# Block 2's gated product over its accumulator in PSUM, rounded and split from there

## The reference

```python
h = rms_norm(x, norm_ffn_g[i])
a, b = jnp.split(h @ w_ffn_in[i], 2, axis=-1)
x = x + ((jax.nn.silu(a) * b) @ w_ffn_out[i]).astype(x.dtype)
```

## Time and profile before

| | |
|---|---|
| median of the runs | 2480.93 us |
| lowest, highest | 2478.26, 2481.35 us |
| profiled execution | 2478.87 us, span 2477.1 us |
| PE busy | 2179.5 us, 88% of the span |
| DVE busy | 739.9 us, 30% |
| ACT, POOL busy | 1089.7, 1606.8 us |
| mean granted clock of TensorE | 0.944 |

### The profile page before, as it was taken

How to read it: one execution, slowest core, us unless ns; L and a number is a source line. 1 busy time by engine, 2 the same in 40 slices (tenths; PEclk the granted TensorE clock), 3 DMA queues, 4 the chain that set the end, 5 groups by cost and what they waited for, 6 DMA issues and landing times.

```text
span 2477.1 us, 39464 instructions
## 1 busy us (share of the span) xinstructions
PE 2179.5 (88%) x13078; PEld 1925.1 (78%) x13078; DVE 739.9 (30%) x1595; ACT 1089.7 (44%) x2051; POOL 1606.8 (65%) x1281
## 2 busy tenths in 40 slices
PE   6698799997779799959998988899899998987997
PEld 6588699786768599749777877799697687776996
DVE  2221344036440344033221153221141310542221
ACT  3344465454134355434442364444344423653543
POOL 5285688881267488849784414699697853236996
PEclk9899899997989999979999899899899998998999
DMA  6533355531024255455435311455354345223553
GB/s 218 119 136 136 100 173 171 199 137 68 1 92 153 97 165 176 153 179 184 149 144 168 128 69 69 136 172 187 138 180 161 136 158 170 69 69 102 175 189 123
DMA packets 217288, 343.66 MB, mean 139 GB/s; under 512 B 8417, under 2 KB 124217, under 8 KB 216955
## 3 DMA queue, kind: packets, MB, share of 16 engines
q1 hardware_dynamic: 206059, 331.59, 39.0%
q10 hardware_dynamic: 11024, 9.45, 1.8%
HBM read 336.83 MB, written 4.19 MB: 138 GB/s over the span
## 4 chain that ended last, share of the span: by engine, by line
PE 75%; issue 6%; DVE 5%; DMA 4%; PEld 3%; ACT 2%; POOL 1%; DVEq 1%; PEldq 1%; ACTq 1%; SPq 0%; POOLq 0%
PE bank L669 11%; PE bank L672 11%; PE bank L673 11%; PE bank L687 7%; PE bank L691 7%; PE bank L690 7%; PE bank L711 3%; PE bank L714 3%; PE bank L715 3%; DMA ring<-in_w_in 2%; DMA distance_table<-PT 1%; PE bank L762 1%; PE bank L833 1%; POOL w_lo L1311 1%; PE bank L792 1%
## 5 line engine op out<-in xcount | busy, mean ns | idle before, releaser
L1311 POOL TENSOR_TENSOR w_lo<-ring,w_hi 128x512 fp32r<-128x512 f32 x1184 | 1548.3, 1321 | 660.3 <-ACT w_hi L1400 596.1
L1400 ACT ACTIVATE w_hi<-ring 128x512 fp32r<-128x512 f32 x1184 | 740.0, 631 | 958.2 <-PE bank L669 395.8
L669 PE MATMUL bank<-x_hi,w_hi 128*128 128x256 f32 x2080 | 602.6, 290 | 49.7 <-DVE x_lo L1829 21.1
L672 PE MATMUL bank<-x_lo,w_hi 128*128 128x256 f32 x2080 | 599.9, 288 | 0.0
L673 PE MATMUL bank<-x_hi,w_lo 128*128 128x256 f32 x2080 | 599.6, 288 | 0.0
L669 PEld LDWEIGHTS bank<-x_hi,w_hi 128*128 128x128 f32 x2080 | 411.6, 198 | 54.1 <-issue 31.1
L672 PEld LDWEIGHTS bank<-x_lo,w_hi 128*128 128x128 f32 x2080 | 411.9, 198 | 0.0
L673 PEld LDWEIGHTS bank<-x_hi,w_lo 128*128 128x128 f32 x2080 | 411.1, 198 | 0.0
L687 PE MATMUL bank<-w_hi,x_hi 128*128 128x512 f32 x720 | 293.2, 407 | 33.5 <-POOL w_lo L1311 13.7
L690 PE MATMUL bank<-w_lo,x_hi 128*128 128x512 f32 x720 | 287.1, 399 | 0.0
L691 PE MATMUL bank<-w_hi,x_lo 128*128 128x512 f32 x720 | 286.7, 398 | 0.0
(11 more groups left out here) (287 smaller groups left out, 2355.5 us busy)
## 6 DMA issues: line engine op xcount, KB each, us to landing
ring<-in_w_in SPq DMA_DIRECT2D x72, 1024.0 KB, 7.1
ring<-in_ffn_w_up SPq DMA_DIRECT2D x44, 1024.0 KB, 7.5
ring<-in_w_ffn_in SPq DMA_DIRECT2D x44, 1024.0 KB, 7.4
ring<-in_ffn_w_down SPq DMA_DIRECT2D x20, 1024.0 KB, 6.0
ring<-in_w_ffn_out SPq DMA_DIRECT2D x20, 1024.0 KB, 6.2
ring<-in_xattn_wkv SPq DMA_DIRECT2D x16, 1024.0 KB, 6.3
ring<-in_w_o_ret SPq DMA_DIRECT2D x16, 1024.0 KB, 6.0
ring<-in_od_w_in SPq DMA_DIRECT2D x12, 1024.0 KB, 6.3
```

What stands on the lines that cost most here:

```text
L669: m = mm(out_, view(w_hi)[:, k, :], x_hi[:, 4 * kh + k, :], start=p % 2 == 0 and k == 0, stop=False)
L672: mm(out_, view(w_hi)[:, k, :], x_lo[:, 4 * kh + k, :], start=False, stop=False)
L1311: tt(view(w_lo), src, view(w_hi), ALU.subtract).then_inc(w_lo_ready, 1)
L1400: return A(o, i_, ACT.Copy, **kw)
```

## The change

In block 2 the product is written over the linear half in its own bank. The rounding and the remainder read it there. The bank is given free by the remainder, not by the product, and `ff_h` by a one-element copy behind a third drain. Block 1 is as before, and `g_s` is only read by DVE.

```diff
--- before.py
+++ after.py
@@ -2319,8 +2319,14 @@
                     B.wait_full(dve, (f"2up{j}", 1))
                     b = B.uses[(f"2up{j}", 1)][0]
                     g = g_s[j % 2][:, 0:2, :]
-                    tt(g, bank[b][:, :].rearrange("p (a b) -> p a b", a=2), g, ALU.mult).then_inc(empty[b], 1)
-                    split_hidden(g, g_hi, g_lo, j)
+                    product = bank[b][:, :].rearrange("p (a b) -> p a b", a=2)
+                    tt(product, product, g, ALU.mult)
+                    drain()
+                    nc.vector.tensor_copy(g_hi[:, 2 * j:2 * j + 2, :], product)
+                    drain()
+                    tt(g_lo[:, 2 * j:2 * j + 2, :], product, g_hi[:, 2 * j:2 * j + 2, :], ALU.subtract).then_inc(empty[b], 1)
+                    drain()
+                    nc.vector.tensor_copy(small[:, 22, 0:1], small[:, 23, 0:1]).then_inc(ff_h, 1)
                 residual_rows("2down")
             B.i = None
             final_norm(12, 32)
```

## The result

The changed kernel took 2486.3 us, the median of 11 runs (2485.55 to 2490.35), against 2480.0 for the kernel before (11 runs, 2478.03 to 2484.38). The forecast was 2485.5. The ratio is 1.0025, with a 95% interval of 1.0016 to 1.0034: slower by 6.3 us, between 4.0 and 8.4. The profiled execution has a span of 2484.5 us where that of before had 2477.1.

What follows compares the result with a forecast made beforehand. PE was taken to bound the kernel, so only its waits count. Two later bank releases (3.06 us) and one clock fall (1.5) gave +4.6 us on a median of 2480.93: 2485.5 us, range 2481.5 to 2489.0.

Steps and rivals of the forecast that it cites:

- Where the cost sits: Block 2, entry of the down projection: PE waits for bank 3 from unit 10's product, once per layer, twice in all.
- rival 4: Block 2's down projection: PE's restart held by something else, bank wait paid in part, 1.15 us per layer, 2483.2; chance 0.03.
- The size of the pause: Ahead of block 2's down projection: bank 3 free 1.53 us later per layer, 3.06 us in all, pause 2.87 us.
- The clock: Behind block 2's two longer pauses: fall to 1.2 GHz, somewhat over one half each, one likeliest, 1.5 us per fall.
- rival 3: Block 2's up units: PE really waits for POOL, so freeing POOL makes it faster, 20 us at most, 2461; chance 0.03.
- The sum: Whole kernel: 3.06 us of later releases plus 1.5 for one clock fall, +4.6 us, 2485.5 us.

Runs made afterwards that it cites:

- experiment 1: Changed kernel with the old form (product in SBUF, bank freed by the product) for unit 10 alone: 2480.79 us, ratio to before 1.0004.
- experiment 2: Kernel before with block 2's product in a bank of its own, accumulator's bank freed by the product: 2480.43 us, ratio to before 1.0007.
- experiment 3: Kernel before with only the third drain and the copy that gives ff_h added in each unit: 2478.79 us, ratio to before 1.0005.
- experiment 4: Changed kernel with four one-element copies, each behind a drain, between remainder and bank release in every unit: 2492.37 us, ratio to before 1.0052.
- experiment 6: Changed kernel with PE taking each bank of the row projections only ahead of its own first matmul: 2474.14 us, ratio to before 0.9974.
- experiment 5: Kernel before with PE taking each bank of the row projections only ahead of its own first matmul: 2469.31 us, ratio to before 0.9956.
- experiment 12: Kernel before with the product in its own bank and row projections' banks taken one by one: 2470.35 us, ratio to before 0.9962.
- experiment 7: Kernel before with five one-element copies, each behind a drain, after every block 2 unit's remainder: one run, 2483.83 us.

## Why the prediction was right, point by point

**Where the cost sits.** Right. The product of unit 10 is on the path through bank 3, and nothing else of DVE's is: experiments 1, 2 and 3 leave out the late release and stand at ratios of 1.0004, 1.0007 and 1.0005; experiments 4 and 6 lengthen and move it, and the pause follows. The rival with a restart held by POOL (rival 4) wanted 1.15 us more per layer and 1.55 to 1.59 came, and experiment 5 starts the down projection without any pause.

**The size of the pause.** 1.53 us more was forecast per layer; it is 1.59 and 1.55 (2.93 less 1.34 and 1.38). The chain of three is 2.23 us (1709.90 to 1712.13), where block 1's row gave 2.22, and the restart behind it takes 0.59 us, where 0.55 was taken over from before. Together 3.1 us.

**The clock.** Right in kind and nearly in size. "Somewhat over one half" for each pause is four of eight in the profiles, one fall per execution in the mean, as the forecast had it; eight cases are few, and the exact hit is luck. A fall costs 1.3 to 1.4 us here, where 1.5 was taken over from block 1, whose falls were counted as 8 matmuls. The matmuls' pace at 2.4 GHz is 0.233 us and not 0.231, which changes nothing.

**The relief of POOL (rival 3).** The relief came, 1745 down to 1311 ns for POOL's slowest and 10.8 us less of DVE in all, where some 12 were forecast. The gain of this rival did not: experiments 2 and 12, and 128.1 to 129.3 us for the up units with and without it. The Trainium skill (SBUF — State Buffer, SBUF: two separate sides) states that a VectorE operation with two SBUF inputs and a GpSimd operation that reads SBUF lock each other out. The traces agree: DVE's remainder takes 1548 ns from SBUF and 692 from a bank. But neither engine was on the path.

**The sum.** 2485.5 us was forecast and 2486.3 measured. Part of that nearness is luck: the forecast stands on a median of 2480.93 from three runs, and eleven runs gave 2480.0. Over the kernel before it is +4.6 against 6.3 (4.0 to 8.4). The terms as they were measured give 3.1 us of pauses and 1.35 of clock, 4.5 in all, so 1.8 us are missing from the sum.

The profiles show where they lie. The stretch that counts runs from the first matmul of 2up0 in the first layer to the end of the span. The kernel before, then the changed one:

```profile
1580.10 0.55 PE L669 MATMUL bank<-x_hi,w_hi 128*128 128x256 f32 x1 [5.18 <-issue]
```

```profile
1581.28 0.55 PE L669 MATMUL bank<-x_hi,w_hi 128*128 128x256 f32 x1 [5.18 <-issue]
```

With spans of 2477.1 and 2484.5 us the stretch takes 897.0 and 903.2 us. In the six profiles where unit 10's product frees bank 3, with the projections as before (the kernel before twice, experiments 1, 2, 3 and 7), it takes 896.8 to 900.4, 898.6 in the mean. In the four of the changed kernel it takes 903.2 to 905.5, 904.8 in the mean. That is the 6.3 us again, and the two groups do not touch. Beside the pauses and the falls behind them, 0.3 us of it is PE's pause at the turn of the loop and 1.4 lies between that and the second down projection. There the clock falls in all four of the changed kernel's executions at a place where it does in one of the six others. The windows lie over the same matmuls, before and after:

```profile
2202.00:2205.20 3.20, 3.20 (x15) 2.61 (x16) 0.00 (x0) 1.28 (x3) 2.76 (x3) 1.00 0.00 0
```

```profile
2206.20:2209.40 3.20, 3.20 (x8) 2.52 (x9) 0.00 (x0) 0.63 (x1) 2.12 (x2) 0.50 0.00 0
```

So most of the missing term is the clock in other places, which the forecast put at nothing. It is not shown that the later release brings these falls: experiment 4 releases later still, has none at that place, and its stretch is 907.1 us, 8.5 over the mean, less than the 9.7 of its own pauses and falls. The rest of its 12.9 us lies ahead of the stretch or is scatter between executions.

No change was given 0.57 and slower 0.41, with 0.2% as the line between them; the ratio of 1.0025 is past it. The size was forecast well, the side of that line was not the one held likelier.

## What to carry to other kernels

An accumulator that is read once more is held once more: ask who takes that bank next and when, at the last turn of the loop above all, since the turns before it had a unit of work as cover and the last one has none. Where a stage takes several buffers, take each ahead of its own first use; that was worth more here (10 us over six projections) than anything done to the engine that gives them back. Cost a pause of PE with the clock behind it: here 1.35 us behind 2.93 where it fell, and 2.4 behind 3.84. And compare two profiles over the stretch that the change can touch: what lies ahead of it scattered by more than the effect.

## What the runs showed of the hardware that was not expected

- A pause of the same length (2.93 us) is followed by 1.2 GHz in four cases of eight. Pauses of 1.34 to 1.40 us at this place never were, in twelve cases; 3.83 and 3.84 both were, and there the fall slowed 12 matmuls where it slowed some 7 behind 2.93. The cost went from 1.35 to 2.4 us.
- DVE's idle time at the turn of the loop is 4.6 to 6.0 us over all these profiles, and neither 11 nor 55 more copies ahead of the branch moved it out of that scatter. PE's pause between the layers takes one of three values: 7.13 us in one profile, 8.20 or 8.21 in ten, 9.41 to 9.43 in three. It does not follow DVE's time one to one (8.21 with 4.95, 8.20 with 5.55), and why it goes in steps is not known.
- One execution of the kernel before took 2484.23 us with nothing changed, 4 us over its median. Most of it arose early: its first matmul of 2up0 starts 3.3 us later than in the first profile. Over the ten profiles compared above that matmul starts between 1576.65 and 1584.58 us, though no instruction ahead of it differs. Only the medians of many runs carry a verdict on the whole time.
